# Gate products with both parts of h as one operand of 512 columns, the product of gate and up on GpSimd, and the squares of q ahead of the decay chain

## What is computed

```python
# block 1, per layer
h2 = rms_norm(x, norm2_g)
x = x + (jax.nn.silu(h2 @ ffn_w_gate) * (h2 @ ffn_w_up)) @ ffn_w_down
# block 2, per layer, twice
def swiglu(h, w_in, w_out):
    gate, up = jnp.split(h @ w_in, 2, axis=-1)
    return (jax.nn.silu(gate) * up) @ w_out
x = post_add(x, swiglu(pre(x, 0), ffn_w_in[l, 0], ffn_w_out[l, 0]), 0, FFN_RES)   # FFN_RES = 0.5
# block 1, delta rule
q, k = l2_normalize(q), l2_normalize(k)
g = -exp(a_log) * softplus(a_in + dt_bias)        # summed along a chunk, and used as exp(g_i - g_j)
mod = silu(c) @ mod_w[l] + mod_b[l]               # 9216 values per layer of block 2
```

## Time and profile before

| | |
|---|---|
| median of 3 runs | 2012.13 us (2011.47 to 2013.09) |
| profiled execution | 2015.44 us |
| its span, first to last instruction | 2013.7 us |
| mean granted clock of TensorE | 0.976 |
| busy: PE, PEld (weight loads) | 1902.3, 1783.2 us |
| busy: DVE, ACT, POOL | 1452.9, 1001.9, 234.9 us |
| L1223 (w_lo) on DVE | 572 instructions, 739.7 us |
| L1331 (mod) on DVE | 128 + 16 instructions, 150.7 + 18.9 us |
| L1713 (g_lo) on POOL | 140 instructions, 191.1 us, mean 1.367 us |

### The profile page before, as it was taken

The page is one execution under the profiler, slowest core; times in us unless marked ns, Lnnn a source line. Parts: engine busy times, 40 slices in busy tenths (PEclk is TensorE's granted clock), DMA queues, the critical chain, the costliest instruction groups (busy, mean ns, idle before and its releaser), DMA issues.

```text
span 2013.7 us, 34482 instructions
## 1 busy us (share of the span) xinstructions
PE 1902.3 (94%) x14192; PEld 1783.2 (89%) x14192; DVE 1452.9 (72%) x2203; ACT 1001.9 (50%) x1621; POOL 234.9 (12%) x182
## 2 busy tenths in 40 slices
PE   6799999979999998999899989998999899989998
PEld 5799899978989997999799979997999889989998
DVE  4565689866566987788777776998677677776555
ACT  5444544464354445545644555445545654455444
POOL 0220111111102110211100001111111100001111
PEclk9899999989999998999999999999999999999999
DMA  5223599622238973556443347894555433344452
GB/s 221 95 87 117 211 351 350 222 88 97 92 105 333 359 290 130 236 201 239 188 147 121 143 157 313 343 368 169 178 178 182 164 126 127 120 174 149 173 184 102
DMA packets 53293, 384.07 MB, mean 191 GB/s; under 512 B 5904, under 2 KB 6032, under 8 KB 6928
## 3 DMA queue, kind: packets, MB, share of 16 engines
q1 hardware_dynamic: 53136, 381.86, 50.7%
HBM read 380.79 MB, written 1.05 MB: 190 GB/s over the span
## 4 chain that ended last, share of the span: by engine, by line
PE 81%; DVE 10%; ACT 5%; issue 4%; DMA 0%; DVEq 0%; SPq 0%; ACTq 0%
PE stream L476 16%; PE stream L477 16%; PE stream L478 16%; PE works L490 5%; PE works L491 5%; PE works L492 5%; DVE w_lo L1223 2%; DVE mx L1331 2%; ACT w_hi L920 2%; PE stream L550 1%; PE stream L551 1%; PE stream L552 1%; DVE mx L1372 1%; PE works L838 1%; DVE x L1311 1%
## 5 line engine op out<-in xcount | busy, mean ns | idle before, releaser
L1223 DVE TENSOR_TENSOR w_lo<-raw,w_hi 128x1024 fp32r<-128x1024 f32 x572 | 739.7, 1310 | 180.3 <-ACT w_hi L920 154.2
L476 PE MATMUL stream<-h_hi,w_hi 128*128 128x256 f32 x2976 | 851.9, 286 | 4.9 <-DVE w_lo L1223 4.8
L477 PE MATMUL stream<-h_lo,w_hi 128*128 128x256 f32 x2976 | 844.8, 284 | 0.0
L478 PE MATMUL stream<-h_hi,w_lo 128*128 128x256 f32 x2976 | 844.6, 284 | 0.0
L920 ACT ACTIVATE w_hi<-raw 128x1024 fp32r<-128x1024 f32 x572 | 591.1, 1051 | 106.8 <-PE works L492 72.7
L476 PEld LDWEIGHTS stream<-h_hi,w_hi 128*128 128x128 f32 x2976 | 573.9, 193 | 12.0 <-issue 8.9
L477 PEld LDWEIGHTS stream<-h_lo,w_hi 128*128 128x128 f32 x2976 | 573.9, 193 | 1.8
L478 PEld LDWEIGHTS stream<-h_hi,w_lo 128*128 128x128 f32 x2976 | 573.4, 193 | 0.0
L1713 POOL TENSOR_TENSOR g_lo<-hid,g_hi 128x256 fp32r<-128x256 f32 x140 | 191.1, 1367 | 1544.9 <-ACT g_hi L950 1544.9
L1125 ACT ACTIVATE gate_t<-stream 128x256 f32<-128x256 f32 x132 | 50.7, 384 | 414.7 <-PE stream L478 406.9
L490 PE MATMUL works<-w_hi,g_hi 128*128 128x512 f32 x480 | 187.7, 391 | 3.3 <-DVE w_lo L1223 3.2
(11 more groups left out here) (454 smaller groups left out, 2199.6 us busy)
## 6 DMA issues: line engine op xcount, KB each, us to landing
raw<-w SPq DMA_DIRECT2D x294, 1024.0 KB, 4.9
mx<-w SPq DMA_DIRECT2D x64, 1024.0 KB, 7.4
par<-p_in SPq DMA_DIRECT2D x2, 1110.0 KB, 7.5
x<-x_in SPq DMA_DIRECT2D x1, 1024.0 KB, 6.8
mx<-bt_in SPq DMA_DIRECT2D x2, 512.0 KB, 6.3
out<-x SPq DMA_DIRECT2D x4, 256.0 KB, 2.6
con<-const_in SPq DMA_DIRECT2D x1, 780.0 KB, 4.8
par<-p_in SPq DMA_DIRECT2D x1, 225.0 KB, 6.9
```

The lines of the kernel that those rows point to most:

```text
L476: mm(o, hi, r_hi[:, kt, :], start=first, stop=False, skip_group_check=True)
L477: mm(o, hi, r_lo[:, kt, :], start=False, stop=False, skip_group_check=True)
L478: last = mm(o, lo, r_hi[:, kt, :], start=False, stop=end, skip_group_check=True)
L1223: v.tensor_tensor(w_lo[:, q % SLOTS, :], raw[:, chunk_of_unit[q] % RAWS, (q % 2) * UNIT:(q % 2 + 1) * UNIT], w_hi[:, q % SLOTS, :].bitcast ...
```

## The change

1. h_hi and h_lo become halves of one buffer h_two, side by side for each k tile. In gu steps `wide_step` replaces three matmuls of 256 columns by one of 512 (w_hi against both parts) and one of 256 (w_lo against h_hi). Gate and up take a whole bank each, of which the left half holds hi x hi + lo x hi and the right half hi x lo.
2. The halves are added outside: ACT copies the two right halves into sq (L1170), DVE adds the left halves (L1539) and frees the banks, ACT takes the tanh from sq (L1173), DVE multiplies (tanh + 1) x gate (L1545), POOL multiplies by up into hid (L1796), ACT rounds g_hi (L991), POOL makes g_lo (L1761). The factor 0.5 moves out of hid: acc scales by 0.5, post takes 4 EPS.
3. stream, stat and turned become one tensor `quad` of four banks, of which each gu takes two in turn. So rows (grow), kzero and bzero use the two banks whose turn it is and wait for them; grow stands one step later, kzero and bzero elsewhere in COEFS; the transposes of pre 0 and pre 2 go to works.
4. ACT rounds one unit of weights ahead of the copy, DVE makes that unit's w_lo between its add and its multiply.
5. nsum 0 stands ahead of decay 0, in both layers of block 1.

```diff
-     ("silu", 1), ("pair", 6), ("gsum", 0), ("lead", 2), ("pair", 2), ("decay", 0), ("nsum", 0), ("lead", 3), ("silu", 2),
+     ("silu", 1), ("pair", 6), ("gsum", 0), ("lead", 2), ("pair", 2), ("nsum", 0), ("decay", 0), ("lead", 3), ("silu", 2),
...
+            def wide_step(unit, o, kt):
+
+                slot = unit % SLOTS
+                hi = w_hi[:, slot, kt * P:(kt + 1) * P]
+                lo = w_lo[:, slot, kt * P:(kt + 1) * P]
+                mm(o, hi, h_two[:, kt, :, :], start=kt == 0, stop=False, skip_group_check=True)
+                return mm(o[:, 0:T], lo, h_hi[:, kt, :], start=False, stop=kt == DT - 1, skip_group_check=True)
...
+                        if i == 7 and n["row"] > 0:
+                            pe.wait_ge(s_row_done, 2 * n["row"])
...
-                    f(gate_t[:, n["g"] % 2, :], bank[:, 0, :], ACT.Tanh, scale=0.5).then_inc(s_gate_th, 1)
                     if i < FT - 1:
                         round_weights(n["split"] + 5)
+                    act.wait_ge(s_unit_done, n["split"] + 2)
+                    f(sq[:, n["g"] % 2, :].rearrange("p (b t) -> p b t", b=2), parts[:, :, 1, :], ACT.Copy)\
+                        .then_inc(s_wide_sb, 1)
+                    act.wait_ge(free, n["pair"] // 2 + 1)
+                    f(gate_t[:, n["g"] % 2, :], sq[:, n["g"] % 2, 0:T], ACT.Tanh, scale=0.5).then_inc(s_gate_th, 1)
                     round_g(n["g"], i % 4)
...
-                    link(v.scalar_tensor_tensor(gate_t[:, g % 2, :], gate_t[:, g % 2, :], 1.0, bank[:, 0, :], ALU.add,
-                                                ALU.mult))
-                    v.scalar_tensor_tensor(hid[:, g % 2, :], gate_t[:, g % 2, :], 0.5, bank[:, 1, :], ALU.mult,
-                                           ALU.mult).then_inc(s_hid_done, 1)
+                    dve.wait_ge(s_wide_sb, n["gu"] + 1)
+                    v.tensor_tensor(both.rearrange("p (b t) -> p b t", b=2), both.rearrange("p (b t) -> p b t", b=2),
+                                    parts[:, :, 0, :], ALU.add).then_inc(free, 1)
+                    if i < FT - 1:
+                        low_weights(n["split"] + 5)
+                    dve.wait_ge(free, n["pair"] // 2 + 1)
+                    dve.wait_ge(s_gate_th, n["gt"] + 1)
+                    v.scalar_tensor_tensor(gate, gate, 1.0, both[:, 0:T], ALU.add, ALU.mult).then_inc(s_gated, 1)
...
-                    low_g(n["g"], i % 4)
+                    g = n["g"]
+                    pool.wait_ge(s_gated, n["gu"] + 1)
+                    v.tensor_tensor(hid[:, g % 2, :], gate_t[:, g % 2, :], sq[:, g % 2, T:2 * T], ALU.mult)\
+                        .then_inc(s_hid_done, 1)
+                    pool.wait_ge(s_hid_done, g + 1)
+                    low_g(g, i % 4)
```

More of the change, by code:

```diff
@@ L49 @@
 COEFS = [("coef", 0), ("coef", 1), ("coef", 2), ("coef", 3), ("coef", 4), ("table", 0), ("coef", 5), ("table", 1),
-         ("coef", 6), ("coef", 7), ("kzero", 0), ("table", 2), ("coef", 8), ("table", 3), ("coef", 9), ("table", 4),
-         ("bzero", 0), ("table", 5), ("table", 6), ("table", 7)]
+         ("coef", 6), ("coef", 7), ("table", 2), ("kzero", 0), ("coef", 8), ("table", 3), ("coef", 9), ("bzero", 0),
+         ("table", 4), ("table", 5), ("table", 6), ("table", 7)]
 RAW_MODS = {2 + 4 * k: k for k in range(8)}
@@ L103 @@
     + [s for k, step in enumerate(ffn_order()) for s in
-       [step] + [("grow", 0)] * (k == 7) + [c for at, c in zip(COEF_STEPS, COEFS) if at == k]]
+       [step] + [("grow", 0)] * (k == 8) + [c for at, c in zip(COEF_STEPS, COEFS) if at == k]]
     + [("post", 0), ("pre", 1)] + MIXER
@@ L165, in numbered @@
 def numbered():
-    n = dict(split=0, pair=0, stat=0, turn=0, bank=0, row=0, h=0, g=0, gt=0, sq=0, x=0, y=0, mod=0)
+    n = dict(split=0, pair=0, stat=0, turn=0, bank=0, row=0, h=0, g=0, gt=0, gu=0, sq=0, x=0, y=0, mod=0)
     out = []
@@ L248, in build @@
         cum_r = sb("cum_r", [P, 2, 384], F32R)
-        stream = [ps(f"stream{i}", [P, 2, T]) for i in range(2)]
+        quad = ps("quad", [P, 4, 512])
+        stream = [quad[:, 2 * i, :].rearrange("p (a t) -> p a t", a=2) for i in range(2)]
         works = ps("works", [P, 4, 512])
@@ L277, in turned_into, with wide, row_banks @@
         def turned_into(B, kind, i):
-            return work if (B, kind, i) == (1, "norm", 1) else [stat, turned, work[0], work[1]]
+            return work if (B, kind, i) in ((1, "norm", 1), (2, "pre", 0), (2, "pre", 2)) else [stat, turned, work[0], work[1]]
+        def wide(n):
+            s = 2 * (n["pair"] % 2)
+            return quad[:, s, :], quad[:, s + 1, :]
+        def row_banks(B, i, n):
+            return (stat, turned) if (B, i) == (2, 1) else wide(n)
         def turned_tile(into, kt):
@@ L602, in _ @@
                         pe.wait_ge(s_mods_done, L + 1)
-                    for half, dst in enumerate((stat, turned)):
+                    if (B, i) != (2, 1):
+                        pe.wait_ge(banks[n["pair"] % 2], n["pair"] // 2)
+                    for half, dst in enumerate(row_banks(B, i, n)):
                         for j in range(4):
@@ L807, in _ @@
                     pe.wait_ge(bt_ld, 16 * (L + 1))
-                    pe.wait_ge(s_row_done, 2 * n["row"])
+                    pe.wait_ge(banks[n["pair"] % 2], n["pair"] // 2)
                     for st in range(ST):
                         ut, q = st // 4, st % 4
-                        o = stat[32 * q:32 * q + 32, 32 * ut:32 * ut + 32]
+                        o = wide(n)[0][32 * q:32 * q + 32, 32 * ut:32 * ut + 32]
                         mm(o, bt[:, 0, 32 * st:32 * st + 32], cp[:, 0, 0, st, :], start=True, stop=False,
@@ L818, in _ @@
                     pe.wait_ge(s_b0t_done, L + 1)
-                    pe.wait_ge(s_k0_sb, 4 * (L + 1))
-                    for e, dst in enumerate((turned, stat)):
+                    pe.wait_ge(banks[n["pair"] % 2], n["pair"] // 2)
+                    for e, dst in enumerate(wide(n)):
                         for ut in range(4):
@@ L965, in _ @@
                     round_weights(n["split"] + units + 2)
-                    if kind not in ("lead", "down", "out", "mout"):
+                    if kind not in ("lead", "gu", "down", "out", "mout"):
                         act.wait_ge(s_unit_done, n["split"] + units)
@@ L1001, in _ @@
                 elif kind == "grow":
-                    for half, src in enumerate((stat, turned)):
+                    for half, src in enumerate(row_banks(B, i, n)):
                         act.wait_ge(s_pe_row, 2 * n["row"] + half + 1)
@@ L1318, in _ @@
                         src = after_out[q] if i == 1 else after_down[q]
[L1319 removed]
+                        v.scalar_tensor_tensor(chunk(x, q), src[:], 1.0 if i == 1 else 0.5, chunk(x, q), ALU.mult,
+                                               ALU.add).then_inc(s_x_done, 1)
                 elif kind == "mod":
```

52 lines of the change are left out of this document (35 added, 17 removed).

## The result

| | before | after |
|---|---|---|
| median | 2012.61 us (2011.47 to 2016.43) | 2128.75 us (2124.40 to 2134.41) |
| ratio | | 1.0575, interval 1.0542 to 1.0608 |
| span of the profiled execution | 2013.7 us | 2132.6 us |

The change makes the kernel 116 us slower. I had forecast 56 us more, and a range that ended at 2098 us: the sign was right, the size was under half of it.

A forecast was written before the change was run, and what follows sets the result against it. PE was taken to bound the kernel (busy 94%), DVE a close second. Products -26, squares of q -16 and stalls +98 gave +56 us, put on the median of 2012.13: 2068 us, range 2032 to 2098.

The forecast's parts named there:

- the chain: In gu steps, from DVE's gate multiply through POOL's product, ACT's g_hi and w_hi back to DVE: 2.33 us.
- the end of an FFN: Last gu reaches g_lo 4.4 us after PE, under the 5.46 us down step: 0, or 1 us each.
- The products themselves: Gate and up matmuls on PE: 0.3473 instead of 0.360 us per k tile, 2112 tiles, 26 us less.
- the merge saves nothing: Rival 3, gu matmuls on PE: 26 us longer, stalls 16 us shorter, 2078 us; chance 0.05.
- The wait in the gu step: DVE's second weights wait 2.33 us for ACT's w_hi; DVE's gu step becomes 5.7 us instead of 3.85.
- The stalls inside the FFNs: PE stalls for DVE in the five FFNs with fillers, none in the last: +98 us, between 66 and 120.
- priced at 0 as hidden: Row products, kzero and bzero in quad banks: wait on a bank left two gu steps ago, hidden, 0.
- My 11 us for the odd tables: Block 2's first FFNs: four waits behind odd tables, where ACT changes its table twice; 11 us per FFN.
- Squares of q: Norm sums ahead of decay in block 1: 8 us per layer, -16 us, between 10 and 18.
- The rival of contention: Rival 2: no wait, but POOL collides with DVE in gu steps, 0.63 us each; 1990 us, chance 0.06.
- The rival of the clock: Rival 4: stalls in the FFNs let PE's clock fall, some 5 us per FFN; 2093 us, chance 0.06.

The follow-up runs named there:

- x4: e6 with hi x h again as two matmuls of 256 columns; 2011.08 us, ratio 0.9987.
- e6: e1b with POOL's product of gate and up cut to 16 of its 256 columns, all waits kept; 1997.64 us, ratio 0.9939.
- e1a: Changed kernel, with ACT rounding the second w_hi ahead of g_hi in each gu step except an FFN's last; 2045.99 us, ratio 1.0161.
- e3: Changed kernel with the product of gate and up on DVE instead of POOL, second w_hi still rounded behind g_hi; 2098.38 us, ratio 1.0434.
- x2: Changed kernel with a copy in place of ACT's sine in the eight odd table steps, so ACT keeps its table; 2131.05 us, ratio 1.0585.
- x1: Changed kernel, with ACT rounding both units of the last down step ahead of g_hi, in each FFN's last gu only; 2119.83 us, ratio 1.0532.
- e2: Kernel before with only the squares of q (nsum 0) put ahead of the decay chain; 2004.98 us, ratio 0.9957.
- e1b: e1a, plus both units of the last down step rounded ahead of g_hi in each FFN's last gu; 2043.33 us, ratio 1.0157.

## Why the prediction had the sign and missed the size

The mechanism was right: the chain, the wait and the engine that waits are those of the forecast. The step that failed is the end of an FFN, a term put at "0, or 1 us each" that measured 29 us in the six; three more terms had the wrong size. Against the sum of the prediction (-26 - 16 + 98 = +56 us), in the order of its parts:

- **The products themselves: -26, measured -12.5.** What was wrong is the price of a k tile, 0.2273 + 0.120 us. I took the 512-column row from a run of equal matmuls. In the changed kernel a k tile takes 5.645 / 16 = 0.353 us against 0.360 before. The rival "the merge saves nothing" was as near as my number. By the gap of columns / 2.4 + 2.5 ns that the page "TensorE: Matmul & The Clock Gate" of the Trainium skill, section "Back-to-back issue gap", gives, an estimate would be 5 us; x4 against e6 lies between that and my 26.
- **The wait in the gu step: 2.33 us, measured 2.25.** Right, and shown: e1a removes the order that makes it and 83 us go; e3 shortens the chain by the amount worked out and 28 us go. Periods with three mods were forecast at 20.6 us; in the second FFN three in a row take 20.1 to 20.3.
- **The stalls inside the FFNs: +98, measured 108** (124.7, plus the 12.5 of the merge, less the 29 of the next point; so it is what is left over, the clock included). By FFN, with the same subtraction: 16.9, 18.4, 36.1, 22.9, 13.9, 0.1, against 20.5, 19.6, 22.6, 27.5, 7.6, 0. The three with mods alone came out 9 us under, the two with tables 20 over: that 98 lies so near 108 is in part luck. What is in those 20 is read, not tested: waits of 8.0 us in the first FFN of block 2 where PE needs a bank that ACT has not yet emptied (the rows with mx L1045 and mx L1201 above and 1.9 of "issue"), which I had priced at 0 as hidden; and its clock, 0.94 in the window against 0.98. My 11 us for the odd tables had the right wait but the wrong cause (x2). How much of the 20 is clock is only bounded. In layer 0's first FFN of block 2, which holds 13.5 of them, matmuls that start at over one and a half times their usual distance, with no wait between, cost 8 us ahead of its end, against 4 before; so the clock gives at most some 4 us of the 13.5.
- **The end of an FFN: "0, or 1 us each", measured 29 us in six.** From the start of the next to last down step to the next stage, the six took 19.1, 24.3, 20.8, 20.2, 19.5 and 20.8 us, against 13.1, 17.2, 17.0, 15.3, 15.8 and 17.3 before. By the starts of the 512-column matmuls in them, some 17 of the 29 us are waits, and some 12 are matmuls at half rate behind the wait ahead of L525 (granted clock 0.82 to 0.91 in these stretches, 0.95 to 1.00 before). This is the largest of the misses, and the step that failed. I followed the last gu to g_lo, found 4.4 us and a cover of 5.5, and overlooked that the two units of the last down step are rounded behind the same g_hi, then need two w_lo. The chain I had described for every other step also ends the FFN, where no later step repays it. x1 returned 8 us of it in the trace; with the rounding early, the collision keeps much of the rest.
- **Squares of q: -16, measured -8** (e2; and 5.8 us outside the FFNs in the changed kernel). The start of lead 3 was forecast at 58.3 us and came at 58.49 in e2, but that is luck, for pair 2 also ended 1.8 us earlier there. Counted from the end of pair 2, lead 3 starts 4.7 us earlier in either layer, not 6.7, since the decay products moved into the stretch at the lower clock, which I left out; and at the next norm sums the gain is 4.8 and 4.2 us, where I had 8.
- **The rival of contention** (0.06) described another kernel than this one, but the right effect: once DVE no longer waits, it is there and costs up to 46 us (e1b against e6), not the 20 that I gave it. I had priced a collision at 0.63 us and counted one for each POOL instruction. In e1b one product is late by a microsecond (1.71 us for 0.73), and with it g_hi and g_lo; and it delays the DVE instruction behind it by half of one.
- **The rival of the clock** (0.06): the clock did fall with the stalls. In the windows of the six FFNs it stood at the lower level for some 86 us, against 48 before. But the matmuls that start far apart without a wait cost 29 us there against 18: some 11 us more, not the 25 of the rival, and they lie behind the wait at the end of each FFN.

The four differences, 13.5 + 10 + 29 + 10 us, make up the 63 between +56 and the 118.9 by which the span grew. As the stalls are what the other terms leave over, the sum closes by construction. A slip in the range changes nothing: the terms named for its ends give 2034 and 2096 us, not 2032 and 2098.
